# Routing of a two-layer diffusion backbone: row numbers of the first expert step by small products, slots of its output weights, idle products, a six-block spill loop

## What is computed

```python
def hier_moe(h, wg, bg, we, be, w1, w3, w2):
    g_logits = hf @ wg + bg                      # 4 groups
    _, g_sel = lax.top_k(g_logits, 1)
    p_group = take_along_axis(softmax(g_logits), g_sel)
    e_logits = (hf @ we + be)[group g_sel]       # 8 experts in the group
    top_p, top_i = lax.top_k(softmax(e_logits), 2)
    weights = p_group * top_p / sum(top_p)
    # per token and chosen expert e:  weight * (silu(x @ w1[e]) * (x @ w3[e])) @ w2[e]
```

## Time and profile before

| | us |
|---|---|
| median of three runs | 2463.81 |
| the profiled execution's own time | 2463.27 |
| its span | 2461.4 |
| PE busy in the span | 2313.6 |
| DVE, ACT, POOL busy | 768.4, 418.8, 280.7 |
| mean granted clock of PE | 0.972 |
| time that the queue of SP's loads and stores was served, share of 16 DMA engines | 55.1% |

### The profile page before, as it was taken

The page is one execution under the profiler, slowest core; times in us unless marked ns, Lnnn a source line. Parts: engine busy times, 40 slices in busy tenths (PEclk is TensorE's granted clock), DMA queues, the critical chain, the costliest instruction groups (busy, mean ns, idle before and its releaser), DMA issues.

```text
span 2461.4 us, 28375 instructions
## 1 busy us (share of the span) xinstructions
PE 2313.6 (94%) x10444; PEld 1164.1 (47%) x10444; DVE 768.4 (31%) x1753; ACT 418.8 (17%) x912; POOL 280.7 (11%) x341
## 2 busy tenths in 40 slices
PE   6989999999996999999998999999996999999987
PEld 3546547888554344443333444444553444443332
DVE  3694114555537111111113511111345111111115
ACT  1301233444121101110102200000111101110111
POOL 0000103223122100000000000000232000000000
PEclk9999999999997999999999999999996999999999
DMA  9881000000316999999897210102207999999986
GB/s 386 297 349 58 0 1 1 2 19 19 125 55 257 387 419 414 418 413 409 357 418 278 87 51 26 51 26 88 91 35 298 419 419 416 419 407 410 374 346 256
DMA packets 146797, 572.28 MB, mean 232 GB/s; under 512 B 25033, under 2 KB 50793, under 8 KB 103914
## 3 DMA queue, kind: packets, MB, share of 16 engines
q1 hardware_dynamic: 133418, 536.97, 55.1%
q0 software_dynamic: 13248, 33.57, 3.6%
HBM read 549.51 MB, written 35.65 MB: 238 GB/s over the span
## 4 chain that ended last, share of the span: by engine, by line
PE 81%; DMA 7%; DVE 6%; SPq 2%; issue 2%; POOL 1%; ACT 1%; DVEq 0%; POOLq 0%; ACTq 0%
PE bank L1091 23%; PE bank L1165 13%; PE bank L1113 11%; PE bank L707 8%; PE bank L1014 4%; PE bank L974 4%; PE bank L664 3%; PE bank L810 3%; DVE lnwb L1525 2%; DMA bigA<-in_moe_w 2%; PE bank L1194 2%; SPq L445 2%; PE bank L824 1%; PE bank L793 1%; DMA bigC<-in_moe_w 1%
## 5 line engine op out<-in xcount | busy, mean ns | idle before, releaser
L1091 PE MATMUL bank<-bigA,bigB 128*32 128x512 f32 (+2 forms) x2048 | 524.9, 596 | 0.0
L1165 PE MATMUL bank<-bigB,bigA 128*128 128x512 f32 x768 | 331.6, 595 | 2.0 <-ACT bigB L1244 2.0
L1091 PEld LDWEIGHTS bank<-bigA,bigB 128*32 128x32 f32 (+2 forms) x2048 | 187.1, 141 | 299.1 <-issue 297.0
L707 PE MATMUL bank<-bigC,bigB 128*128 128x512 f32 (+3 forms) x768 | 292.4, 536 | 0.0
L1113 PE MATMUL bank<-bigA,bigB 128*32 128x512 f32 (+2 forms) x992 | 259.2, 612 | 14.8 <-DMA bigA<-in_moe_w 11.8
L1165 PEld LDWEIGHTS bank<-bigB,bigA 128*128 128x128 f32 x768 | 146.5, 191 | 186.6 <-issue 186.6
L707 PEld LDWEIGHTS bank<-bigC,bigB 128*128 128x128 f32 x768 | 142.4, 192 | 127.6 <-issue 119.5
L1244 ACT ACTIVATE bigB<-bank,small 128x128 f32<-128x128 f32 x288 | 107.5, 460 | 381.7 <-PE bank L664 381.7
L1091 PE MATMUL bank<-bigC,bigB 128*32 128x512 f32 (+2 forms) x640 | 163.2, 594 | 0.0
L1113 PEld LDWEIGHTS bank<-bigA,bigB 128*32 128x32 f32 (+2 forms) x992 | 91.4, 143 | 142.3 <-issue 138.2
L2150 POOL DMA_INDIRECT y_rows<-bigB,ints x44 | 44.5, 1011 | 909.0 <-DVE bigB L1936 909.0
(11 more groups left out here) (286 smaller groups left out, 2279.7 us busy)
## 6 DMA issues: line engine op xcount, KB each, us to landing
bigA<-in_moe_w SPq DMA_DIRECT2D x292, 1024.0 KB, 20.6
bigC<-in_moe_w SPq DMA_DIRECT2D x92, 1024.0 KB, 22.9
bigA<-in_ada_w SPq DMA_DIRECT2D x40, 1024.0 KB, 7.4
bigA<-y_rows SPq DMA_DIRECT2D x16, 1024.0 KB, 4.9
bigA<-in_w_in_odd SPq DMA_DIRECT2D x24, 512.0 KB, 6.2
bigA<-in_ada_w SPq DMA_DIRECT2D x4, 2048.0 KB, 12.5
bigC<-in_w_in_even SPq DMA_DIRECT2D x4, 2048.0 KB, 14.3
h_rows<-bigC SPq DMA_DIRECT2D x16, 512.0 KB, 4.8
```

What stands on the lines that cost most here:

```text
L707: last = mm(bank(n % 3)[:, 0:w], uT[:, k, t * P:(t + 1) * P], wring[:, g % 2, k, at_:at_ + w], start=(k == 0), stop=(k == KC - 1))
L1091: last = mm(bank(m)[at_:at_ + w, :], xT[:, j, KC // 2 * h + k, at_:at_ + w], w13_at(SLOT_OF[m, h, q][0], k), start=(h == 0 and k == 0), st ...
L1165: last = mm(bank(3 * half + m), wc[:, j, m, k, :], u1T[:, k, half * 512:(half + 1) * 512], start=(k == 0), stop=(k == KC - 1))
```

## The change

In the routing PE now forms the rank first and the counts behind it. From the rank alone DVE computes the lanes of experts 0 and 1 (`first_key`, and `first_is`, one instruction of 128 x 1024), and 8 products give the rows of step 0 (`first_row`, `first_tok`), which POOL gathers while the rest of the routing goes on. ACT alone scales and shifts the rows of step 0. The table's products stand between step 0's first and second products; the one-hot matrices come from four wide instructions in place of 32. The rows of step 1 are gathered behind the table, and transposed behind step 0's second products.

`freed` now takes the four slots of step 0's output weights as free ahead of those of step 1's first products. Pieces 10 and 11 wait for the first gather. `fill(b, n)` is n products of 128 x 512 that nobody reads, at several places. The spill loop has 4 turns of 6 blocks, and its count is loaded ahead of the steps. SP loads the first two residual tiles ahead of the last output, and the first `pair` in two halves; `gate_rows(2)` stands ahead of the first combination, and DVE's `gate_diag` inside the last step.

```diff
 def freed(piece):
     m, h, q = piece
-    return (LAST[q], 2 * m + h) if m < 2 else (LAST[q] + 1, 4)
+    return (LAST[q], 2 * m + h) if m < 2 else (LAST[q] + (LAST[q] > 0), 4)
...
-OVER = 24
+OVER, OVER_TURN = 24, 6
...
-        lane_is = at(bigB, 2048, 16, P)
-        step_is = at(bigB, 6784, 16, TABLE)
+        lane_is = [at(bigB, 1024, NT, P), at(bigB, 3072, NT, P)]
+        step_is = at(bigB, 7392, 16, TABLE)
+
+        first_key, first_is = bigB[:, 6200:6216], at(bigB, 3072, NT, P)
...
+        def run_over(eng, n_over, block_):
+
+            with eng.Fori(0, OVER // OVER_TURN) as i:
+                with eng.If(OVER_TURN * i < n_over):
+                    for j in range(OVER_TURN):
+                        block_(OVER_TURN // 2 * i + NB // 2 + j // 2, j % 2)
...
                 if n == AFTER_ROUTER:
-                    sp.wait_ge(S("route_mm"), 7 * l + 2)
+
+                    sp.wait_ge(S(f"xg_in{l}_0"), 16)
+                    sp.wait_ge(S("route_mm"), 8 * l + 2)
...
-                if n == PREFETCH + 2:
-
-                    sp.wait_ge(S(f"xg_in{l}_0"), 16)
...
-                for n in range(EARLY[l], AFTER_ROUTER):
+                for n in range(EARLY[l], 8):
                     piece(l, n)
                 store(NT - 1)
                 ln_params(l, 1)
-                for n in range(AFTER_ROUTER, len(PIECES)):
+                for n in range(8, len(PIECES)):
                     piece(l, n)
...
-                sp.wait_ge(S(f"h_mm{l}"), 4 * NB)
-                sp.wait_ge(S(f"y_mm{l}"), NB)
+                sp.wait_ge(S(f"h_mm{l}"), 4 * NB - 2)
                 for t in range(2):
                     load(hback[:, t], h_dram[l][t * P:(t + 1) * P, :], f"x_in{t}")
...
+                    if t == 0:
+                        load(pair[:, 0, :, 0:512], rows[:, :, 0:512], "pair_in0")
+                        load(pair[:, 0, :, 512:], rows[:, :, 512:], "x_in2")
...
+            def fill(b, n):
+
+                for _ in range(n):
+                    mm(bank(b), cc("ones"), cst[:, 0:512], start=True, stop=True, skip_group_check=True)
...
             def last_rows(l):
 
+                pe.wait_ge(S("res"), l * NT + NT - 1)
+                fill(0, 2)
                 rows_T(l, NT - 1)
+                fill(0, 1)
                 logits(l, NT - 1)
...
             def moe(l):
 
+                fill(0, 6)
+                pe.wait_ge(S("routed"), 8 * l + 1)
...
+                fill(0, 1)
+                pe.wait_ge(S("routed"), 8 * l + 2)
+                for t in range(NT):
+                    last = mm(bank(1)[:, 0:2], first_is[:, t, :], cc("rown")[:, t:t + 2], start=(t == 0), stop=(t == NT - 1))
+                last.then_inc(S("route_mm"), 1)
...
-                gathered_T(0, 0, 1)
-                gathered_T(1, 1, 1, 6)
-                for b in range(NB):
+                fill(0, 5)
+                gathered_T(0, 0, 1, 6)
+                fill(0, 1)
+                hidden_half(0, 0)
+                table()
+                hidden_half(0, 1)
+                gathered_T(1, 1, 1)
+                n_over = over_count(pe, l)
+                for b in range(1, NB):
                     hidden_half(b, 0)
-                    if b:
-                        gated_T(b - 1)
+                    gated_T(b - 1)
                     hidden_half(b, 1)
-                    if b:
-                        gathered_T(b + 1, (b + 1) % 2, (b + 1) // 2 + 1)
-                        output(b - 1)
+                    gathered_T(b + 1, (b + 1) % 2, (b + 1) // 2 + 1)
+                    output(b - 1)
...
+            gate_rows(2, diag1[:, 0], 2)
             for t in range(NT):
                 combined(0, t)
-                if t < 2:
-                    gate_rows(t + 2, diag1[:, t], (2, 6)[t])
+                if t == 0:
+                    gate_rows(3, diag1[:, 1], 6)
                 if t:
                     stream_T(t - 1)
+            fill(4, 2)
             stream_T(NT - 1)
+            fill(4, 1)
...
+                V(v.scalar_tensor_tensor(first_key.rearrange("p (t e) -> p t e", t=NT), rank[:, :, 0:2], 1.0,
+                                         chosen.rearrange("p (t e) -> p t e", t=NT)[:, :, 0:2], ADD, MUL))
+                V.wait()
+                v.tensor_tensor(first_is[:, :, :].rearrange("p t (e s) -> p (t e) s", e=2),
+                                wide(cc("iota")[:, 1:65].unsqueeze(1), [P, 2 * NT, 64]),
+                                wide(first_key.unsqueeze(2), [P, 2 * NT, 64]), ALU.is_equal).then_inc(S("routed"), 1)
+                dve.wait_ge(S("route_mm"), 8 * l + 4)
...
+                dve.wait_ge(S("route_mm"), 8 * l + 5)
+                V(v.tensor_scalar(first_row, bank(1)[:, 0:1], float(ROWS), None, ADD))
+                V.wait()
+                v.tensor_scalar(first_tok, first_row, 1, None, ALU.arith_shift_right).then_inc(S("routed"), 1)
...
-                for c in range(16):
-                    v.tensor_scalar(lane_is[:, c, :], cc("iota"), lane_f[:, c:c + 1], None, ALU.is_equal)
-                    v.tensor_scalar(step_is[:, c, :], cc("iota")[:, 0:TABLE], step_f[:, c:c + 1], cc("rown")[:, c:c + 1],
-                                    ALU.is_equal, MUL).then_inc(S("spot"), 1)
...
-                gather(0, tok[:, 0:1])
+                gather(0, first_tok)
+                pool.wait_ge(S("routed"), 8 * l + 7)
                 gather(1, tok[:, 1:2])
```

More of the change, by code:

```diff
@@ L238, in program @@
         tok, rows_of = ints[:, 0:TABLE], ints[:, TABLE:2 * TABLE]
+        first_row, first_tok = ints[:, 194:195], ints[:, 195:196]
         gidx = ints[:, 100:102]
@@ L372, in program, with over_count @@
         ctx_tiles = [(NT, NT + 1), (NT + 1, NT)]
[L374 to L381, removed]
+        def over_count(eng, l):
+            eng.wait_ge(S("routed"), 8 * l + 8)
+            return eng.value_load(ov[0:1, OVER + 1:OVER + 2], min_val=0, max_val=OVER)
+        def run_over(eng, n_over, block_):
[3 more added lines that the diff above has]
+                        block_(OVER_TURN // 2 * i + NB // 2 + j // 2, j % 2)
         groups = [(0, 512), (512, 512), (2048, 288), (1536, 512), (1024, 512)]
@@ L1192, in combined @@
                 for n in range(2):
+                    if t == 0 and n:
+                        pe.wait_ge(S("x_in2"), 48 + 16 * (l + 1))
                     for k in range(2):
@@ L1389, in gated @@
                     go(gT[:, 0:2, :].rearrange("p k i -> p (k i)"), bank(4)[:, 0:256], ACT.Copy).then_inc(S(f"gT_ev{l}"), 1)
-                rows_T(0, 0)
-                rows_T(1, 1, 6, "u_ev")
-                for b in range(NB):
-                    if b:
-                        act.wait_ge(S(f"g_d{l}"), b)
+                act.wait_ge(S(f"x_T{l}"), 1)
+                modulated(parts(xT[:, 0]), 6, mod_of(l, 1), f"xT_ev{l}")
+                modulated(parts(xT[:, 0]), 6, mod_of(l, 1), f"xT_ev{l}", 4, KC)
+                silu(0)
+                rows_T(1, 1)
+                n_over = over_count(act, l)
+                for b in range(1, NB):
+                    act.wait_ge(S(f"g_d{l}"), b)
                     silu(b)
-                    if b:
-                        gated(b - 1)
-                        rows_T(b + 1, (b + 1) % 2)
+                    gated(b - 1)
+                    rows_T(b + 1, (b + 1) % 2)
                 gated(NB - 1)
@@ L1943, in scattered @@
                     output(b % 2)
-                rows_T(0, 0)
-                rows_T(1, 1, 6, "u_ev_d")
-                for b in range(NB):
-                    if b:
-                        gated(b - 1)
-                    gate_up(b)
-                    if b:
-                        rows_T(b + 1, (b + 1) % 2)
-                        scattered(b - 1)
+                gate_up(0)
+                rows_T(1, 1)
+                n_over = over_count(dve, l)
+                for b in range(1, NB):
+                    gated(b - 1)
+                    gate_up(b)
+                    rows_T(b + 1, (b + 1) % 2)
+                    if l == 0 and b == NB - 1:
+                        gate_diag(diag1[:, 0], 4 + 2)
+                        gate_diag(diag1[:, 1], 4 + 5)
+                    scattered(b - 1)
                 gated(NB - 1)
@@ L1965, in block_of @@
                     output(j)
[L1967 to L1970 removed]
+                run_over(dve, n_over, block_of)
             def combined(l, t):
```

106 lines of the change are left out of this document (56 added, 50 removed).

## The result

The changed kernel takes 2482.65 us (median of 4 runs, 2482.07 to 2485.0) against 2463.92 for the kernel before; the ratio is 1.0081, with a 95% interval of 1.0065 to 1.0097. It is 18.7 us slower. The forecast was 2468.6 with a range up to 2477: the sign is right, the size is not.

What follows compares the result with a forecast made beforehand. Each expert stage was taken as bound by the weight stream up to a long PE wait and by PE behind it. 2463.27 + 15.4 (expert stages) - 10.1 (both ends) = 2468.6 us; range 2460 to 2477.

Steps and rivals of the forecast that it cites:

- What bounds the kernel: Expert stages: weight stream sets the time up to a PE wait of 26.2 and 25.9 us, PE behind it.
- The first rows: Routing: `first_tok` at 783 and gather 0 landed at 789.3, 14 us earlier than before.
- PE behind it: Steps 0 and 1, layer 0: products from 793.4, gather 1 out at 805.9, step 1 from 817.8, 4.5 us earlier.
- The slots: Expert stages: piece 24 waits for `output(0)` until 840.4, the stream runs dry; 7.7 us later per layer, together +15.4.
- the late hole: Layer 0's stream: nothing to load from 829.4 until piece 24 arrives at 842.7, 13.3 us.
- The early hole: Layer 0's routing: the stream empty for 4.9 us, up to 791.9 when pieces 10 and 11 arrive.
- The ends: Ends of both layers and the convolution's clock: 7.2 us saved in layer 0, 2.9 in layer 1, together -10.1.
- the half pair: End of a layer: half of the first pair of rows loads in 3.4 to 3.5 us in place of 4.74.
- Rival 1: Expert stages: the stream never runs dry, `output(0)` comes at some 832; faster, 2444 us; chance 0.12.
- Rival 2: Gather 1 passes the backlog, landing 6.5 us behind its issue, 3 us less a layer; about 2463; chance 0.15.
- Rival 3: Clock is half throughout the routing, step 1 and `output(0)` 4 us later in each layer; 2477; chance 0.15.
- Rival 4: Ends save little: scatter takes 5.4, halves land no earlier than the whole, the clock stays; 2473; chance 0.10.

Runs made afterwards that it cites:

- g_clock: The changed kernel plus three idle products while PE waits for the second gather and one behind its transposes; 2480.58 us.
- f_whole: a_slots with the first pair of rows loaded whole in place of in two halves; 2443.83 us.
- h_turn: a_slots with the spill loop in 12 turns of two blocks in place of 4 turns of 6; 2449.6 us.
- a_slots: The changed kernel with step 0's output-weight slots again free only behind step 1's products, plus three small moves of loads and buffers; 2443.9 us.

## Why the prediction was right or wrong

**What bounds the kernel** was read rightly in its main point: a hole in the stream moves the last wait, and the table shows it more sharply than the forecast used it. Its reading of the earlier trace rows was wrong. The 26.2 and 25.9 us are the time from a piece's issue to its landing; PE stood still for 4.47 us there in layer 0 and for 3.82 in layer 1, not for 26. So PE had far less slack than the prediction's "waits 26 us later" says. That did no harm to the sum, since PE's late `output(0)` acted through the stream.

**The first rows** came as summed: `first_tok` at 784.1 (forecast 783), the gather out at 785.0, landing 4.8 us later at 789.8 (789.3).

**PE behind it** is where most of the size was lost. The sum had the transposes begin as the gather lands; they stood behind five idle products until 792.0. It had 7.0 for the first half of step 0; it took 8.74, at a granted clock of 0.50 from 796 to 799, behind 2.14 us in which PE had idled for ACT's scaling. So gather 1 went out at 809.7 (805.9). Its landing was priced well (9.0, forecast 9.5). Step 1 started at 821.6 (817.8). Then the sum took 22.3, a step at full clock, up to the end of `output(0)`; it took 25.4 (846.99 - 821.58). Of these 3.1 us, 2.5 are the first half, which took 9.61 in place of 7.09: the granted clock was 0.50 from 821.6 to 826, behind pauses of 3.34 and 1.60 us. With four idle products in those pauses it took 7.09 (g_clock). The other 0.6 is the step itself, 22.8 us at full clock in g_clock. The forecast was 840.1, the truth 847.0. I had costed the idle products at nothing because they "lie beside the gather's flight": in place of that cover they outlasted it by 2 us.

**The slots.** The mechanism was the forecast's main one and holds. The stream ran dry within a microsecond of the 829.4 in the sum. The term was mis-sized: 7.7 in layer 0, measured 15.2. By the DMA share, the late hole was 19.1 and not 13.3, 5.8 more, as `output(0)` ended 6.9 later. I had counted the hole of the kernel before as 9, a mean of bytes and share, where the share has 7.5: 1.5 more. I had taken off 1.5 as absorbed, and nothing is absorbed. The early hole was 1.2 shorter than summed (3.7 for 4.9), which is on the other side. Together 7.6, and the last wait shows 7.5. (The sum also has a slip of 0.2: 840.4 + 2.1 is 842.5, not 842.7.) Layer 1 was given 7.7 and cost 11.4; its stream was empty for 13 us more. Together 25.8 us from the last output products, where the sum had 15.4, beyond my bound of 20.

**The ends** were forecast at -10.1 and gave -6.8. Layer 0 up to the convolution's start 3.5 and the convolution's clock 1.7, together 5.2 for 7.2; layer 1 1.6 for 2.9. The first product of the combination came 10.2 us behind the last output of layer 0 (1335.67 - 1325.51), where the forecast had 10.1. The step that failed is the half pair at 3.5 us. In the chain of the changed kernel the second half lands 7.44 us behind its issue, with one more load of `y_rows` and others issued behind it, and the tile's last products wait for it until 1339.30:

```profile
1327.62 3.51 DMA y_rows<-bigB,ints
...
1331.82 7.44 DMA bigA<-y_rows
...
1341.69 5.95 DMA bigA<-h_rows
```

The whole pair took 4.74. Loading it whole helps the first tile and not the end, as f_whole shows: PE then waits for `hback` of the third tile, which the sum didn't look for. The Trainium skill's fit for a gpsimd transfer ("DMA: Bandwidth & Descriptors", anatomy of one DMA) would have given 3.2 for the half. With a second and a third load behind it in the queue neither it nor my row said anything of 7.44. The spill loop's gain is real (5.7 by h_turn). In the kernel before SP's turns did end last, as I had it; with SP's loop moved ahead, as in h_turn, PE's turns and the half clock behind them cost as much.

**The rivals.** Rival 1, that the stream never runs dry, was priced at 2444 and stated as a question of when `output(0)` ends. Its condition failed in the change itself, as its "against" said. a_slots, in which piece 24 no longer waits for that output, measured 2443.9, but that the two agree to 0.1 is luck. The rival's 9 us for the stages came from a step 1 that starts 4.5 us earlier; in a_slots it starts at 822.20, as before, and the stages gain 11.9 and the ends with the convolution 7.9, where the rival had 9 and 10.1. Rival 2 is refuted: gather 1 took 9.0 us beside a full stream. Rival 3 holds in part and by another way than I had it: the clock was 1.00 from 765 to 775 and 0.50 from 780 to 785, and it was half in part of the first half of step 1 (0.67 over 820 to 830) and of step 0's, on the path to `output(0)`. It should have been a term of the sum and not a rival, since the two pauses of PE, for ACT and for gather 1, could be read off the order of the instructions. Rival 4, that the ends save little, came true for a third of them, 3.3 of 10.1 us; by its sign, the second half landed later than the whole pair had.

The range missed because its upper end took one of these at a time. Late `output(0)`, nothing absorbed and smaller ends are three doubts that all made it slower. Adding them up would not have been enough: the prediction's own bounds, +20 and -5, end at 2478.3, as the expert stages cost 25.8.

## What to carry to other kernels

Where one stream sets the time, add up the microseconds in which it has nothing to load, and count them in full: here each of them moved the last wait by one, in either direction, to within 2 to 5 us over 20. Count the idle time of the engine that waits as well, and not the flight of the transfer that it waits for: it says how much filling the stream can still bring. A queue that is served in order should take its slots in the order in which they really come free; four pieces that wait for a late event cost 27 to 39 us although the slots for pieces behind them came free sooner. And an event that releases the stream deserves the same care as a critical path: here 4.9 us of pauses ahead of step 1 were followed by 2.5 us lost to half clock.

## What was not expected of the hardware

A pause of PE of 2.14 us, and one of 3.34 with 1.60 behind it, were followed by products partly at half clock: 8.74 and 9.61 us for 32 matmuls that take 7.09 elsewhere; with four idle products in the second place it was 7.09. Of two halves of a transfer, issued one behind the other with more loads behind them, the second was complete 7.44 us after its issue; the whole in one transfer took 4.74.
